# Two transformer stacks on one core: the first head of the first tile is scored at the end of the attention heads and routed as soon as the second tile is normed, and expert slots are taken in the order in which they come free

## What is computed

```python
def peer_block(hb, w_q, sub_keys, u_tab, v_tab):
    q = (hb @ w_q).reshape(n, PEER_HEADS, PEER_QDIM)          # 8 heads, 256 wide
    s1 = einsum('nhd,kd->nhk', q[..., :128], sub_keys[0])     # 128 keys a half
    s2 = einsum('nhd,kd->nhk', q[..., 128:], sub_keys[1])
    v1, i1 = top_k(s1, 16);  v2, i2 = top_k(s2, 16)
    top_s, pos = top_k(v1[..., :, None] + v2[..., None, :], 16)
    expert = take(i1 * 128 + i2, pos)                         # 16 of 16384 rows
    w = softmax(top_s) * gelu(einsum('nhkd,nd->nhk', u_tab[expert], hb))
    return einsum('nhk,nhkd->nd', w, v_tab[expert])
```

## Time and profile before

| | |
|---|---|
| median of 3 runs | 3313.51 us (3307.21 to 3314.12) |
| the profiled execution | 3313.55 us, its span 3311.8 us |
| busy share of the span | PE 80%, DVE 55%, POOL 38%, ACT 14% |
| experts' gathers, first to last issued | "latents" 1728.7 to 2369.3 us, "last" 2629.0 to 3266.1 us |

### The profile page before, as it was taken

How to read it: one execution, slowest core, us unless ns; L and a number is a source line. 1 busy time by engine, 2 the same in 40 slices (tenths; PEclk the granted TensorE clock), 3 DMA queues, 4 the chain that set the end, 5 groups by cost and what they waited for, 6 DMA issues and landing times. The chain is left out here.

```text
span 3311.8 us, 26588 instructions
## 1 busy us (share of the span) xinstructions
PE 2640.4 (80%) x8912; PEld 1413.4 (43%) x8912; DVE 1817.9 (55%) x4657; ACT 479.8 (14%) x1401; POOL 1251.7 (38%) x1072
## 2 busy tenths in 40 slices
PE   6786797999987899874877888887867688888876
PEld 2354565764533486331443343333334433334332
DVE  1438557786213166431147676777536577677774
ACT  0210111000101100000111111111112111111111
POOL 0000425452445255445515444454300254445442
PEclk8898886999997899987888998999978899899999
DMA  6656856897878599798839999999751399999996
GB/s 260 258 207 233 299 222 228 295 370 261 293 285 293 190 339 408 293 368 308 287 105 419 419 419 418 421 421 421 322 191 49 123 419 419 418 419 421 421 421 280
DMA packets 249211, 1046.81 MB, mean 316 GB/s; under 512 B 20550, under 2 KB 53430, under 8 KB 176884
## 3 DMA queue, kind: packets, MB, share of 16 engines
q0 software_dynamic: 147456, 805.37, 61.0%
q1 hardware_dynamic: 93456, 222.23, 18.2%
q10 hardware_dynamic: 8164, 17.53, 1.5%
HBM read 1041.28 MB, written 3.77 MB: 316 GB/s over the span
## 5 line engine op out<-in xcount | busy, mean ns | idle before, releaser
L1382 POOL DMA_INDIRECT sb_beside_slots<-in_peer_uv,sb_beside_chosen x256 | 331.3, 1294 | 423.2 <-DVE sb_beside_slots L1282 237.7
L1282 DVE SCALAR_TENSOR_TENSOR sb_beside_slots<-sb_beside_slots,sb_beside_H 128x1024 f32<-128x1024 f32 x256 | 304.8, 1223 | 118.5 <-DMA sb_beside_slots<-in_peer_uv,sb_beside_chosen 87.7
L1382 POOL DMA_INDIRECT sb_beside_slots<-in_peer_uv,sb_beside_small x256 | 250.0, 977 | 245.2 <-PE psum L1339 172.7
L174 PE MATMUL psum<-sb_f_arena,sb_f_ring 128*128 128x256 f32 (+1 forms) x1344 | 296.4, 384 | 9.0 <-issue 9.0
L174 PEld LDWEIGHTS psum<-sb_f_arena,sb_f_ring 128*128 128x128 f32 (+1 forms) x1344 | 251.5, 188 | 54.6 <-issue 13.5
L1339 PE MATMUL psum<-sb_beside_slots,sb_xc 128*32 128x512 f32 x1024 | 163.1, 767 | 123.2 <-DMA sb_beside_slots<-in_peer_uv,sb_beside_small 101.8
L174 PE MATMUL psum<-sb_f_ring,sb_f_arena 128*128 128x512 f32 (+2 forms) x448 | 192.3, 590 | 2.0 <-ACT sb_f_arena L1699 2.0
L1202 PE MATMUL psum<-sb_latents_ring,sb_latents_scores 128*128 128x512 f32 x304 | 152.2, 654 | 51.2 <-ACT sb_latents_scores L1160 51.2
L1202 PE MATMUL psum<-sb_last_ring,sb_last_scores 128*128 128x512 f32 x276 | 139.2, 655 | 47.3 <-ACT sb_last_scores L1160 47.3
L1202 PE MATMUL psum<-sb_beside_slots,sb_latents_scores 128*128 128x512 f32 x288 | 142.2, 641 | 31.9 <-ACT sb_latents_scores L1160 31.9
L2329 PE MATMUL psum<-sb_f_ring,sb_f_arena 128*128 128x512 f32 x384 | 165.4, 593 | 0.0
(11 more groups left out here) (554 smaller groups left out, 4674.3 us busy)
## 6 DMA issues: line engine op xcount, KB each, us to landing
sb_f_ring<-in_w_ff SPq DMA_DIRECT2D x32, 2048.0 KB, 14.1
sb_context_ring<-in_ada_w SPq DMA_DIRECT2D x23, 2048.0 KB, 11.0
sb_f_ring<-in_w_in SPq DMA_DIRECT2D x8, 2048.0 KB, 14.4
sb_f_ring<-in_w_in SPq DMA_DIRECT2D x6, 1904.0 KB, 9.1
sb_context_ring<-in_peer_w_q SPq DMA_DIRECT2D x8, 1024.0 KB, 10.2
sb_f_ring<-in_w_out SPq DMA_DIRECT2D x4, 2048.0 KB, 9.2
sb_latents_ring<-in_peer_w_q SPq DMA_DIRECT2D x8, 1024.0 KB, 17.7
sb_last_ring<-in_peer_w_q SPq DMA_DIRECT2D x8, 1024.0 KB, 16.6
```

The costliest lines, as they stand in the source:

```text
L174: last = e.matmul(out, a, b, start=(i == 0), stop=(i == len(terms) - 1))
L1282: e.scalar_tensor_tensor(out=row, in0=row, scalar=1.0, in1=self.H[:, t, :], op0=ALU.mult, op1=ALU.mult, accum_out=self.dots[t][:, s:s + 1] ...
L1382: e.indirect_dma_start(out=self.slots[i % self.SLOTS], out_offset=None, in_=self.table, in_offset=bass.IndirectOffsetOnAxis(ap=at, axis=0) ...
```

## The change

PE computes turn 0's query halves (g0 only) right after the last head, and its scores after `oT` of g1; ACT keeps the query in the second norm's gain row, which is not needed any more. DVE routes turn 0 right after `second_norm(1)`, and the first gathers are issued from there. Turn 1 is routed after the first two batches of dots. The slots are listed in a new order: those free at the heads' end first, then the ring, last those of the gains and of the modulation rows. `queries(0)`, `queries(1)` and their scores now cover g1 alone.

```diff
     else:
-        order += tail(g1)
+        order += ["qe", ("oT", g1), "se"] + tail(g1)[1:]
...
             transposed(("h2T", g0))
+            early.keep_query(e, gains[:, 1, 0:2 * P])
             transposed(("oT", g1))
             if beside:
                 beside.all_summed(e)
             square_of(1)
             e.dma_start(mod[:, 2, :], rows[0:1, 5, :].to_broadcast([P, D])).then_inc(mods_in[1], 16)
             transposed(("h2T", g1))
+            early.exps(e)
...
             second_norm(1)
+            early.route(e)
             e.wait_ge(mods_in[1], 32)
...
         else:
+            early.queries(e)
             for group in tail(g1):
                 if group[0] == "h2T":
                     mark(5)
                 tail_group(group)
+                if group[0] == "oT":
+                    early.scores(e, gains[:, 1, 0:2 * P])
...
+    def gather(e, n):
+        q, k = n // TOPK, n % TOPK
+        if k == 0:
+            e.wait_ge(idx_ready, q + 1)
+        if n == n_early:
+            e.wait_ge(*front.ring_free)
+        if n == ns - 2:
+            e.wait_ge(*front.normed)
+        if n >= ns:
+            e.wait_ge(added, n - ns + 1)
+        e.indirect_dma_start(out=slots[n % ns], out_offset=None, in_=table, in_offset=bass.IndirectOffsetOnAxis(ap=rt["idx"][:, q % 4, k:k + 1], axis=0),
+                             element_offset=layer * NE * 2 * D).then_inc(row_in[n % ns], 16)
+
+    class Early:
+
+
+        def queries(e):
+            e.wait_ge(wq_in[0], 16)
+            e.wait_ge(*front.st.emptied(("h2T", 0)))
+            e.wait_ge(*front.st.freed("qe"))
+            for b in range(2):
+                done = matmuls(e, front.st.pair("qe")[:, b, 0:P], [(wq_half[0][:, k, b * P:(b + 1) * P], hT[:, k, 0:P]) for k in range(KT)])
+            done.then_inc(front.st.mm, 1)
+
+        def keep_query(e, kept):
+            e.wait_ge(*front.st.computed("qe"))
+            e.activation(kept.rearrange("p (b n) -> p b n", b=2), front.st.pair("qe")[:, :, 0:P], ACT.Copy).then_inc(*front.st.empties("qe"))
+
+        def scores(e, kept):
+            e.wait_ge(*front.st.freed("se"))
+            e.wait_ge(*front.st.emptied("qe"))
+            for b in range(2):
+                done = e.matmul(front.st.pair("se")[:, 0, b * P:(b + 1) * P], kept[:, b * P:(b + 1) * P], sub[:, 2 + b, :], start=True, stop=True)
+            done.then_inc(front.st.mm, 1)
+
+        def exps(e):
+            e.wait_ge(top_ready, 1)
+            e.activation(rt["ex"], rt["tv"], ACT.Exp, bias=rt["nm"], accum_out=rt["z"]).then_inc(exped, 1)
+
+        def gather(e):
+            if beside:
+                e.wait_ge(beside.summed, 3)
+            for n in range(n_early):
+                gather(e, n)
...
+        def route_first(e):
+            e.wait_ge(*front.st.computed("se"))
+            e.tensor_copy(SC[:, 0, 0, :], front.st.pair("se")[:, 0, 0:S]).then_inc(*front.st.empties("se"))
+            e.wait_ge(*front.st.emptied("se"))
+            for half in range(2):
+                route_half(e, own, rt, half, SC[:, 0, 0, half * NK:(half + 1) * NK])
+            route_sums(e, own, rt, top_ready)
+            picks(0)
...
+        Early.route = route_first
+        front.vector(e, Early)
+        for b in range(2):
+            for r in range(BATCH):
+                dot(b * BATCH + r)
+            weights(b)
         keep_scores(0)
         keep_scores(1)
-        for q in (0, 1):
-            half_of(q, 0)
-            half_of(q, 1)
-            route_sums(e, own, rt, top_ready)
-            picks(q)
-            keep_scores(2 + q)
+        half_of(1, 0)
+        half_of(1, 1)
+        route_sums(e, own, rt, top_ready)
+        picks(1)
+        keep_scores(2)
+        keep_scores(3)
         for q in range(len(turns)):
             more = q + 2 < len(turns)
-            for j in range(TOPK // BATCH):
+            for j in range(2 if q == 0 else 0, TOPK // BATCH):
                 b = TOPK // BATCH * q + j
                 for r in range(BATCH):
                     dot(b * BATCH + r)
-                if more and j < 2:
+                if q == 0 and j == 2:
+                    half_of(2, 0)
+                    half_of(2, 1)
+                if q == 0 and j == 3:
+                    route_sums(e, own, rt, top_ready)
+                if q > 0 and more and j < 2:
                     half_of(q + 2, j)
-                if more and j == 2:
+                if q > 0 and more and j == 2:
                     route_sums(e, own, rt, top_ready)
                 if more and j == 3:
                     picks(q + 2)
...
+        weights(0)
         keep_queries(0)
         keep_queries(1)
+        weights(1)
         keep_queries(2)
-        route(0)
         keep_queries(3)
         route(1)
         for q in range(len(turns)):
-            weights(4 * q)
+            if q > 0:
+                weights(4 * q)
             if ahead(q):
                 keep_queries(ahead(q))
-            weights(4 * q + 1)
+            if q > 0:
+                weights(4 * q + 1)
             weights(4 * q + 2)
             if q + 2 < len(turns):
                 route(q + 2)
             weights(4 * q + 3)
...
         scores(0)
+        scores(1)
+        sums(0)
         queries(2)
-        scores(1)
         queries(3)
+        sums(1)
         scores(2)
         scores(3)
         for q in range(len(turns)):
             if ahead(q):
                 queries(ahead(q))
-            sums(4 * q)
-            sums(4 * q + 1)
+            if q > 0:
+                sums(4 * q)
+                sums(4 * q + 1)
             if ahead(q):
                 scores(ahead(q))
...
-    slots = [ring[:, j // 2, 2048 * (j % 2):2048 * (j % 2 + 1)] for j in range(4)] + [work[:, 0:2048], work[:, 2048:4096]]
-    slots += [pair(gains, 0), aux[:, 0:2048], pair(mod, 0), *spare]
+    slots = [*spare]
     if last:
         at = 3584 + ROUTE_COLS
-        slots += [mod[:, 3:5, :].rearrange("p k n -> p (k n)"), pair(H, 1), flat(sb["hT2"][:, :, :], "p k n -> p (k n)")[:, 2048:4096]]
+        slots += [mod[:, 3:5, :].rearrange("p k n -> p (k n)"), pair(H, 1)]
         slots += [big[:, at + 2048 * j:at + 2048 * (j + 1)] for j in range(2)]
+    slots += [work[:, 0:2048], work[:, 2048:4096], aux[:, 0:2048]]
+    sb["n_early"] = len(slots)
+    slots += [ring[:, j // 2, 2048 * (j % 2):2048 * (j % 2 + 1)] for j in range(4)]
+    slots += [flat(sb["hT2"][:, :, :], "p k n -> p (k n)")[:, 2048:4096]] if last else []
+    slots += [pair(gains, 0), pair(mod, 0)]
```

More of the change, by code:

```diff
@@ L757, in gpsimd, with tensor @@
             e.dma_reset()
-    def tensor(e):
+        if early:
+            early.gather(e)
+    def tensor(e, early=None):
         e.wait_ge(par, 64 if context else 48)
@@ L1033, in experts @@
     bank_q, bank_sc = [psum[:, 4 + j, 0:S] for j in range(2)], [psum[:, 6 + j, 0:S] for j in range(2)]
+    first_tile = lambda b: 1 if b < 2 else 0
+    n_early = sb["n_early"]
     u_of = lambda n: slots[n % ns][:, 0:D]
@@ L1046, in sync @@
         e.nop()
-    def gpsimd(e):
-        front.gpsimd(e)
-        if beside:
-            e.wait_ge(beside.summed, 3)
-        for n in range(n_rows):
-            q, k = n // TOPK, n % TOPK
-            if k == 0:
-                e.wait_ge(idx_ready, q + 1)
-            if n >= ns:
-                e.wait_ge(added, n - ns + 1)
-            e.indirect_dma_start(out=slots[n % ns], out_offset=None, in_=table, in_offset=bass.IndirectOffsetOnAxis(ap=rt["idx"][:, q % 4, k:k + 1], axis=0),
-                                 element_offset=layer * NE * 2 * D).then_inc(row_in[n % ns], 16)
+    def gather(e, n):
[10 more added lines that the diff above has]
+                             element_offset=layer * NE * 2 * D).then_inc(row_in[n % ns], 16)
@@ L1060, in gpsimd @@
+    def gpsimd(e):
+        front.gpsimd(e, Early)
+        for n in range(n_early, n_rows):
+            gather(e, n)
         for j in range(ns):
@@ L1064, in vector @@
     def vector(e):
-        front.vector(e)
         own = Tally(dve)
+        def route_first(e):
[6 more added lines that the diff above has]
+            picks(0)
         def keep_scores(b):
@@ L1137, in scalar @@
     def scalar(e):
-        front.scalar(e)
+        front.scalar(e, Early)
         def keep_queries(b):
@@ L1143, in keep_queries @@
                 e.wait_ge(sc_done, b - 1)
-            e.activation(qbuf[b % 2], bank_q[b % 2], ACT.Copy).then_inc(q_copied, 1)
+            at = first_tile(b) * P
+            e.activation(qbuf[b % 2][:, at:], bank_q[b % 2][:, at:], ACT.Copy).then_inc(q_copied, 1)
         def route(q):
@@ L1178, in tensor @@
     def tensor(e):
-        front.tensor(e)
+        front.tensor(e, Early)
         def queries(b):
-            f = b // 2
+            f, at = b // 2, first_tile(b) * P
             e.wait_ge(wq_in[f % 2], 16 * (f // 2 + 1))
@@ L1185, in queries @@
                 e.wait_ge(q_copied, b - 1)
```

(4 more changed lines are left out.)

13 lines of the change are left out of this document (7 added, 6 removed).

## The result

The changed kernel takes 3291.74 us in the median of 7 runs (3281.91 to 3296.3), the kernel before 3313.51 (7 runs). The ratio is 0.9938, with a 95% interval of 0.9922 to 0.9953: faster by about 20.5 us, between 15.6 and 25.8. The profiled execution took 3295.09 us with a span of 3293.3.

What follows compares the result with a forecast made beforehand. Bytes were taken to bound the stage's middle and the chain to gather 0 its start. Gather 0 earlier gives 26.5 us, less 9.0 for loads, so 17.5 us off 3313.55: 3296.0, range 3289 to 3306.

Steps and rivals of the forecast that it cites:

- as summed: Whole kernel: dryness under 1.5 us, loads near their price; 3296, itself 3293 to 3300; chance 0.58.
- half the price of the loads: Rival at the stream's start: loads hide better or `oT` is less late; 3291.5 with half the price; chance 0.16.
- What bounds the stage: In "latents", bytes bound the middle, the chain to gather 0 the start; each microsecond gather 0 comes earlier is won.
- the change doesn't do what it says: Rival: the loop from landing over dot, weights and sum to next gather sets the pace; 3313.5 within 6; chance 0.06.
- `oT` late by 3.4 us: On PE, 32 added product rows between the last head and `oT` delay it by 3.2 to 3.6 us.
- 16.6 us removed, the way from copy to gather kept: From norm to scores 16.6 us go, copy to gather 0 stays 10.7; gather 0 13.1 and 13.4 us earlier.
- Load 3 wholly in the stream, load 2 by half: 4.5 us a stage: Query weight loads moved into the gather stream cost 3.0 and 1.5 us, 9.0 us in both stages.
- The stream doesn't run dry: Gathers 16 and 22 go out with 7 and 4 us to spare; cost nothing, bounds 0 and 5 us a stage.
- The windows that I feared: DMA share between 1750 and 1800: no window under 0.95; a dip there means the second rival.
- the second rival: The stream runs dry for a while at gather 22 or 26, 2 to 5 us a stage; 3300 to 3307; chance 0.17.
- PE's first sums: Ahead of gather 22, `sums(0)` takes 9.97 us and `sums(1)` 7 us; gather 22 is issued near 1772.
- The slower case: Rival: turn 1's indices come so late that DMA stands still, once gather 16 goes out after 1773; chance 0.03.

Runs made afterwards that it cites:

- experiment 1: The changed kernel with the slots in the old order (ring first) and every gather behind both waits; 3290.56 us, ratio 0.9944.
- experiment 5: The changed kernel with 10 idle DVE copies between the second batch of dots and turn 1's routing; 3287.26 us, ratio 0.9934.
- experiment 7: The changed kernel with turn 1 routed ahead of the first two batches of dots, the old order; 3292.62 us, ratio 0.9948.
- experiment 2: The changed kernel with the early query's products and scores placed behind both products of `wo`; 3280.42 us, ratio 0.9911.
- experiment 4: The changed kernel with turn 0 routed on DVE before the second norm and four gathers issued ahead of the norm's power on POOL; 3254.24 us, ratio 0.9835.
- Experiment 3: The changed kernel with only the first 2 of 8 query weight loads a stage, their weights reused for heads 2 to 7; 3256.24 us, ratio 0.9832.
- experiment 6: The changed kernel with 30 idle DVE copies between the second batch of dots and turn 1's routing; 3305.08 us, ratio 0.9984.

## Why the prediction was right

3296.0 was forecast and 3291.74 measured, in the range of 3289 to 3306, faster. By the offsets above, the change is worth 19.2 us where 17.5 was the sum. Experiments 1, 5 and 7 leave gather 0 where it was and stay within the slack, so they measure the same effect again; with the changed kernel's own the four ratios are 0.9938, 0.9944, 0.9934 and 0.9948, in the mean 0.9941 or 19.5 us. That is 3294, inside what "as summed" was to give (3293 to 3300). The median of the changed kernel itself lies 1.3 us under that case, at what half the price of the loads would give (3291.5); the offsets decide between the two, and they charge 7.8 of the 9.0 us. Step by step:

- *What bounds the stage.* Right. A gather 0 that comes 3.4 us earlier (experiment 2), or 20.6 (experiment 4), is found again at the last dot, as 3.7 and 5.0 us (with load 2's part, see there) and as 16.6 and 17.7. Experiments 5 and 7 move gather 16 by +4 to +5 and by -11 to -12 us and the last dot by at most 0.6. The rival "the change doesn't do what it says" (the loop through dot and sum sets the pace) is excluded by these.
- *`oT` late by 3.4 us.* Right: the 32 rows took 3.81 us, `oT` starts 4.52 us after the last head's products instead of 1.05, `wo` 6.67 instead of 3.26, so 3.5 and 3.4. Taking them away (experiment 2) gives `wo` back 3.4 us and gather 0 the same.
- *16.6 us removed, the way from copy to gather kept.* The copy starts 0.08 us before the norm's row ends; from copy to gather 0 it took 10.62 us. Gather 0 came 13.3 and 13.6 us earlier where 13.1 and 13.4 were forecast: 0.4 of the 1.7 us that the sum was short.
- *Load 3 wholly in the stream, load 2 by half: 4.5 us a stage.* The mechanism is right (loads issued at 1709.05 and 1746.54, 1.1 us ahead of gather 0 and 36.3 behind it). The size is the term that was off: 7.8 measured, 9.0 forecast, which is the other 1.2 us. Experiment 3 puts load 2 at 0.9 to 1.4 and a later load at 2.8 to 3.0, so 4.2 in "latents" and 3.9 in "last", 8.1 in all. The 3.0 from the pace of the waits came out nearly right, but in part by luck: it counted loads 4 to 7 between rows 27 and 153, while load 4 was spread over rows 24 to 30, of which only 28 to 30 lie behind row 27. With the 3.4 loads that lie there the same 12.2 us give 3.6 each. The fit in the Trainium skill, "DMA: Bandwidth & Descriptors", section "Anatomy of one DMA", was made on DMAs that gpsimd issues, and these loads are issued by SP; taken over, its term for the bytes gives an estimate of 2.4 us for the megabyte, and by it the two stages came to 7.2. Its total is the nearer one here, but the direct price of a load in the full stream is above it. The stream grew by 3.2 us in "latents" and by 4.6 in "last", but that difference lies with the kernel before, whose own two stages differ by 1.0 in its one profile: in the changed kernel and experiments 1, 5 and 7 both stages take 665.7 to 666.6 us.
- *The stream doesn't run dry.* Right. The windows that I feared for read 1.01 to 1.03. I had computed that gather 16 goes out 38.8 us behind gather 0 and had 7 us to spare; it went out after 37.8 and 37.5, and experiment 6 measured a slack of 6.9 to 7.5 us. For the second rival's 2 to 5 us a stage gather 16 would have had to come 9 to 12 us later.
- *PE's first sums.* `sums(0)` took 9.13 us, and `sums(1)`, behind the two queries, 6.9 to the scores (1746.34 to 1753.21), where 9.97 and 7 were taken. DVE waited 5.85 us ahead of the copy of score 2, as forecast (some 6). Gather 22 of "latents" was issued 57.7 us behind gather 0 against a forecast of 56.4 and a limit of 60.7, without a dip of the share. The experiments delay it only together with gather 16, so its own slack isn't measured.
- *The slower case.* It was to need a gather 16 after 1773, that is 57 us behind gather 0. Experiment 6 has it at 51.2 and 51.5 and lies 5 us under the kernel before. Of the gains of 10.1 and 9.0 us it has lost 6.3 and 6.9, so the gain would be eaten 3.8 and 2.1 us further on, at 55.0 and 53.6, if each further microsecond costs a whole one (no run goes that far); the prediction's 57.4 less the 3.3 that it allowed for the measurement is 54.1.
